# First head of a trunk kernel: pieces in 16 places, a new order of loads, products shared with TensorE, k-steps in two parts

## What is computed

```
a     = silu(c) @ ada_w + ada_b          # shift, scale, gate of each sub-layer
h     = rmsnorm(x, g) * (1 + scale) + shift
q,k,v = split(h @ w_in, 3)               # 8 heads
logit = q @ k.T + rel_table[bucket(j - i)]
```

## Time and profile before

| | us |
|---|---|
| median of 3 runs | 1284.4 (1284.37 to 1286.52) |
| profiled execution, device time | 1283.53 |
| its span in the trace | 1281.7 |
| busy PE | 1234.9 (96%) |
| busy DVE | 695.2 (54%) |
| busy ACT | 562.6 (44%) |
| busy POOL | 528.6 (41%) |

### The profile page before, as it was taken

One profiled execution on the slowest core, in us unless ns is written; L12 is line 12 of the kernel. 1 busy time (PEld: TensorE's weight loads), 2 busy tenths in 40 slices (PEclk: granted clock), 3 DMA queues, 4 the chain that ended last, 5 costly groups with the idle time before them and its releaser, 6 DMA issues.

```text
span 1281.7 us, 16893 instructions
## 1 busy us (share of the span) xinstructions
PE 1234.9 (96%) x5490; PEld 972.4 (76%) x5490; DVE 695.2 (54%) x1175; ACT 562.6 (44%) x899; POOL 528.6 (41%) x265
## 2 busy tenths in 40 slices
PE   4799999989999999999999999999999999999996
PEld 2677777767888888888888777668788888888884
DVE  4756777653676776434444999972533333331002
ACT  4356665663533444342223655663544444442221
POOL 1242333132334444344442677744244444444440
PEclk9799999999999999999999999999999999999999
DMA  9544344422355555234443222202222222232321
GB/s 344 184 145 149 121 140 153 143 99 66 131 196 181 176 183 180 99 109 156 156 166 134 68 66 72 65 27 82 77 89 96 97 90 93 96 109 95 104 87 65
DMA packets 44919, 156.78 MB, mean 122 GB/s; under 512 B 4936, under 2 KB 5192, under 8 KB 44880
## 3 DMA queue, kind: packets, MB, share of 16 engines
q1 hardware_dynamic: 43488, 153.98, 35.4%
q10 hardware_dynamic: 1392, 2.32, 0.6%
HBM read 154.15 MB, written 2.12 MB: 122 GB/s over the span
## 4 chain that ended last, share of the span: by engine, by line
PE 86%; DVE 6%; DMA 3%; issue 2%; ACT 2%; SPq 0%; DVEq 0%; ACTq 0%
PE psum L860 25%; PE psum L862 25%; PE psum L861 25%; PE psum L1126 3%; DMA ada_first<-ada_w 2%; PE psum L895 2%; PE psum L871 1%; DVE pt_lo L1342 1%; DVE psum L1333 1%; PE psum L958 1%; DVE acc L1210 1%; PE psum L907 1%; PE psum L997 0%; PE psum L888 0%; PE psum L985 0%
## 5 line engine op out<-in xcount | busy, mean ns | idle before, releaser
L462 POOL TENSOR_TENSOR w_lo<-w_raw,w_hi 128x1024 fp32r<-128x1024 f32 (+1 forms) x192 | 453.8, 2379 | 707.7 <-ACT w_hi L543 707.7
L860 PE MATMUL psum<-h_hi,w_hi 128*128 128x512 f32 x1152 | 467.1, 405 | 3.8 <-DVE x L1437 2.2
L861 PE MATMUL psum<-h_lo,w_hi 128*128 128x512 f32 x1152 | 449.9, 391 | 0.0
L862 PE MATMUL psum<-h_hi,w_lo 128*128 128x512 f32 x1152 | 449.9, 391 | 0.0
L860 PEld LDWEIGHTS psum<-h_hi,w_hi 128*128 128x128 f32 x1152 | 217.5, 189 | 55.3 <-issue 9.3
L861 PEld LDWEIGHTS psum<-h_lo,w_hi 128*128 128x128 f32 x1152 | 217.3, 189 | 46.9 <-issue 5.3
L862 PEld LDWEIGHTS psum<-h_hi,w_lo 128*128 128x128 f32 x1152 | 216.9, 188 | 46.6
L543 ACT ACTIVATE w_hi<-w_raw 128x1024 fp32r<-128x1024 f32 (+1 forms) x192 | 195.4, 1032 | 73.4 <-DMA w_raw<-w_tiles 73.4
L860 PE MATMUL psum<-a_hi,w_hi 128*128 128x512 f32 x352 | 137.4, 390 | 0.8 <-issue 0.8
L862 PE MATMUL psum<-a_hi,w_lo 128*128 128x512 f32 x352 | 137.0, 389 | 0.0
L861 PE MATMUL psum<-a_lo,w_hi 128*128 128x512 f32 x352 | 137.0, 389 | 0.0
(11 more groups left out here) (184 smaller groups left out, 1361.6 us busy)
## 6 DMA issues: line engine op xcount, KB each, us to landing
w_raw<-w_tiles SPq DMA_DIRECT2D x160, 512.0 KB, 3.3
ada_buf<-ada_w SPq DMA_DIRECT2D x32, 512.0 KB, 3.4
ada_mid<-ada_w SPq DMA_DIRECT2D x32, 512.0 KB, 4.5
w_raw<-w_tiles SPq DMA_DIRECT2D x32, 448.0 KB, 3.1
ada_first<-ada_w SPq DMA_DIRECT2D x16, 512.0 KB, 6.2
ada_late<-ada_w SPq DMA_DIRECT2D x16, 512.0 KB, 4.6
x<-x_in SPq DMA_DIRECT2D x4, 512.0 KB, 10.9
bias<-rel_scratch ACTq DMA_DIRECT2D x1, 2048.0 KB, 8.2
```

Of the source, the lines that this page charges most:

```text
L462: nc.gpsimd.tensor_tensor(w_lo[:, slot, 0:k], w_raw[:, (ph.tile + l) % 2, 0:k], f(w_hi[:, slot, 0:k]), ALU.subtract).then_inc(lo_done, 1)
L860: nc.tensor.matmul(dst, w_hi[:, slot, k], rhs_hi, start=first, stop=False)
L861: nc.tensor.matmul(dst, w_hi[:, slot, k], rhs_lo, start=False, stop=False)
L862: return nc.tensor.matmul(dst, w_lo[:, slot, k], rhs_hi, start=False, stop=last)
```

## The change

It has five parts.
1. The 16 pieces get 16 places (ada_first becomes a list, homes_of_pieces), so no load waits for a buffer. SP issues weight tiles 0 and 1 and x first, then pieces 0 to 7, tables, weight tile 2, pieces 8 to 15, then the bias tiles (moved here from ACT), then tiles 3 to 5.
2. Of chunks 0 and 1, TensorE multiplies k = 1, 3, 5 itself (first_parts, four one-column products for each k, with the piece as weights and a column of cact moving), and DVE the other five. Chunks 2 and 3 stay whole on DVE. DVE now keeps one running sum, in PSUM (FIRST_SUM), and the last addition goes to SBUF. first_product replaces first_ada.
3. DVE adds the squares of x in PSUM, and one 128x512 product sums over partitions instead of eight. ACT splits weight tiles 0 and 1 ahead of the squares, and 1/rms goes to PSUM (OB). The t tiles of the first norm are in PSUM banks 4 and 5.
4. The gain of each half is one instruction (first_gain) instead of two, and first_out takes two chunks in one instruction.
5. Head 0: for k = 0 to 3 all of q, k and v; then the products of chunks 2 and 3, bias tiles 0 and 1; then q and k for k = 4 to 7; then v for k = 4 to 7. DVE does chunks 2 and 3 after the first four norm tiles. All eight bias tiles go through one PSUM bank (FIRST_BIAS), and ACT copies each out (bias_turned) between its other work. The relative bias table's two products follow chunk 1.

```diff
-        first_sums = ((acc[:], v_t[:]), (v_even[:], v_odd[:]))
-        ada_first = at("ada_first", [P, 4, 2, S], F32, qk_base)
+        first_sums = (acc[:], v_t[:], v_even[:], v_odd[:])
...
+        ada_first = [at(f"ada_first{p}", [P, 2, S], F32, o) for p, o in enumerate(homes_of_pieces)]
...
+        PE_PARTS = ((1, 3, 5), (1, 3, 5), (), ())
...
             for t in range(2):
                 load_tile(HEAD, 0, t)
+            for n in range(4):
+                sp.dma_start(x[:, 2 * n:2 * n + 2], x_in[:, 2 * n:2 * n + 2]).then_inc(x_landed[n], 16)
+            for p in range(8):
+                load_first(p)
+            sp.dma_start(tables[:], consts[:, 0:RELS_PAD + 2 * P]).then_inc(consts_in, 16)
+            load_tile(HEAD, 0, 2)
+            for p in range(8, 16):
+                load_first(p)
+            sp.wait_ge(rel_out, 16)
...
+            def first_parts(ch):
+
+                for k in PE_PARTS[ch]:
+                    pe.wait_ge(ada_first_landed[4 * ch + k // 2], 16)
+                    for j in range(4):
+                        nc.tensor.matmul(first_to(ch, j), ada_first[4 * ch + k // 2][:, k % 2, P * j:P * (j + 1)],
+                                         cact[:, k:k + 1], start=(k == PE_PARTS[ch][0]), stop=False)
...
+            first_parts(0)
+            pe.wait_ge(sq_added, DK)
+            nc.tensor.matmul(psum[:, OB], ones[:], rms[:], start=True, stop=True).then_inc(first_sum, 1)
+            first_product(0)
+            first_parts(1)
+            first_product(1)
...
+            def turn_bias(h):
...
+                pe.wait_ge(pt_read, 2 + h)
...
+            for k in range(2, 4):
+                first_qk(k)
+                first_v(k)
+            first_product(2)
+            first_product(3)
+            for h in range(2):
+                turn_bias(h)
+            for k in range(4, DK):
+                first_qk(k)
+                if k < DK - 1:
+                    turn_bias(k - 2)
+            for k in range(4, DK):
+                first_v(k)
+                if k < DK - 1:
+                    turn_bias(k + 1)
...
+            def first_chunk(ch):
...
+                mine = [k for k in range(DK) if k not in PE_PARTS[ch]]
+                for k, after in zip(mine, mine[1:] + [DK]):
...
+                        dve.wait_ge(ada_used, DK * ch + k)
...
+                        V.scalar_tensor_tensor(out=first_sums[ch] if after == DK else psum[:, FIRST_SUM], in0=part,
+                                               scalar=scalar, in1=psum[:, FIRST_SUM], op0=ALU.mult,
+                                               op1=ALU.add).then_inc(ada_used, after - k)
...
+            first_squares()
             dve.wait_ge(act_setup, 1)
             first_chunk(0)
+            first_chunk(1)
             lambda_sums()
...
             norm_tiles(0, 0, DK // 2)
+            dve.wait_ge(h_ready, DK // 2)
+            first_chunk(2)
+            first_chunk(3)
+            first_out(1)
+            first_gain(1)
             norm_tiles(0, DK // 2, DK)
```

More of the change, by code:

```diff
@@ L480, in bias_copy, with mask_add @@
                 nc.gpsimd.tensor_copy(tmps[par][:], tile_of(bias, g)).then_inc(bias_ready, 1)
[L482 to L485, removed]
+            def mask_add(h):
                 pool.wait_ge(pt_read, 3 + h)
@@ L620, in qk_hi_of @@
                 nc.scalar.activation(k_hi[:, par], psum[:, 1], ACT.Copy).then_inc(qk_hi, 1)
+            split_tile(HEAD, 0, 5)
+            bias_turned(4)
             qk_hi_of(0, 0, 0)
-            for h in range(HEADS):
-                act.wait_ge(pt_done, 3 + h)
-                nc.scalar.activation(bias[:, h], psum[:, PT + h % 2], ACT.Copy).then_inc(pt_read, 1)
-                if h == 1:
-                    split_tile(HEAD, 0, 5)
+            for h in range(5, HEADS):
+                bias_turned(h)
             def copy_v(it, c):
@@ L914, in _ @@
-            for ch in range(CH0):
-                first_ada(ch)
+            pe.wait_ge(act_setup, 1)
+            first_parts(0)
[4 more added lines that the diff above has]
+            first_product(1)
+            pe.wait_ge(consts_in, 48)
+            nc.tensor.matmul(psum[0:HEADS, FIRST_BIAS, :], tab[:], onehot[:, 0:S], start=True, stop=True)\
+              .then_inc(pt_done, 1)
@@ new lines, in _, with first_qk @@
+            pe.wait_ge(sc_read, 2)
+            nc.tensor.matmul(psum[0:HEADS, 2, 0:RELS_PAD - S], tab[:], onehot[:, S:RELS_PAD],
+                             start=True, stop=True).then_inc(pt_done, 1)
+            def first_qk(k):
+                pe.wait_ge(h_ready, k + 1)
+                q_last = mm3(psum[:, 0], 0, k, h_hi[:, k], h_lo[:, k], k == 0, k == DK - 1)
+                if k == DK - 1:
+                    q_last.then_inc(q_done, 1)
+                k_last = mm3(psum[:, 1], 1, k, h_hi[:, k], h_lo[:, k], k == 0, k == DK - 1)
+                if k == DK - 1:
+                    k_last.then_inc(k_done, 1)
@@ L936, in head_products @@
                 weights_ready(ph, i2, cc, 3)
[L937 to L938 removed]
+                pe.wait_ge(v_copied, h)
                 for k in range(DK):
@@ L1001, in attention_steps @@
                         10: (lambda: turn_p(3),), 12: (output,), 14: (ada,), 15: (mean_square,)}
-            beside = {DK + k: (lambda h=k: turn_bias(h),) for k in range(DK)}
-            head_products(0, 0, beside)
             with pe.Fori(0, 3) as it:
@@ new lines, in first_out, with two, first_gain @@
+            def first_out(half):
+                def two(t, at_, step):
+                    return t[:, at_:at_ + 2 * step].rearrange("p (a b) -> p a b", a=2)[:, :, 0:4]
+                dve.wait_ge(ada_mm, 2 * (half + 1))
+                V.tensor_tensor(two(mod, DK // 2 * half, DK), first_outs(half),
+                                two(prm, PARAMS["ada_b"] + DK // 2 * half, DK), ALU.add).then_inc(sc_read, 2)
+            def first_gain(half):
+                lo = DK // 2 * half
+                dve.wait_ge(sc_read, 2 * (half + 1))
+                g = PARAMS["norm_g"] + lo
+                V.scalar_tensor_tensor(out=gain[:, 0, lo:lo + 4], in0=mod[:, DK + lo:DK + lo + 4], scalar=1.0,
+                                       in1=prm[:, g:g + 4], op0=ALU.add, op1=ALU.mult).then_inc(dve_step, own.tick())
+                dve.wait_ge(dve_step, own.now())
```

206 lines of the change are left out of this document (109 added, 97 removed).

## The result

The changed kernel is slower than the one before: median 1288.64 us (1286.77 to 1291.27, 10 runs) against 1284.71 us (1282.83 to 1286.58, 10 runs), ratio 1.0031, 95% interval 1.0020 to 1.0042. That is 4.0 us, between 2.6 and 5.4. The forecast was 1283.5 us, with 0.52 on no change and 0.18 on slower. A later comparison of the same two kernels gave 1.0028 (1.0016 to 1.0039).

The account below looks back on a forecast made before the run. PE bounds the kernel, so only an earlier head 1 counts: 71.9 against 72.8, -0.9 us, turns the profiled 1283.53 into 1282.6, and the median 0.9 above it gives 1283.5. The range was 1279.2 to 1287.0.

Parts of the forecast that it names:

- Loads: Start of the kernel: piece 0 lands at 15.9, piece 15 at 37.5, 4 us earlier than before.
- PE before head 0: Chunks 0 and 1 on PE: 32 one-column products at 0.43 plus 1.7, 15.4 us, ending at 31.3.
- first half of the norm: After chunk 1: h complete for k = 0 at 34.3, k = 3 at 38.2; head 0 starts 12.2 us earlier.
- rival 1: Before head 0: PE's clock rises during one-column products, which then cost 0.22; -4.9 us, 1279.5, chance 0.12.
- Chunks 2 and 3: DVE after 38.2: 16 chained instructions 0.78 apart, 12.5 us, ending at 50.7.
- rival 3: Chunks 2 and 3 on DVE: the chain runs at 0.66 an instruction; -2.8 us, 1281.6, chance 0.10.
- The clock in the second half: Second half of head 0: chunk 3's products and first bias tile 1.7 each at low clock, up again at 57.
- Rival 4: Second half of head 0: PE's clock stays low, back later than about 59; +3.1 us, 1287.5, chance 0.18.
- ACT's queue: Before q and k of k = 4: copy 0.60, weight tile 1.04, h_hi 0.76, h_lo 0.81, to 57.4; costs 2 us.
- The rest to head 1: From q and k of k = 4 at 57.4: 14.4 us, and 0.1 for hand-overs, to head 1 at 71.9.
- The mark of before: Head 1's start in the kernel before: 72.8, with three products of v following the last bias product at 71.24.
- rivals 1 to 3: Three faster cases at the start; the second, clock staying high from 45 to 52, gives -2.6 us, 1281.8, chance 0.15.

Follow-up runs that it names:

- experiment 4: Against the changed kernel, ACT splits weight tile 3 before it copies the first bias tile; ratio 1.0032 (1.0018 to 1.0046) to the kernel before.

## Why the prediction was wrong

By its own steps, on the chain's times:

- *Loads, PE before head 0, first half of the norm*: right. 15.9, 31.3 and 34.3 were all met within 0.1, and the end of the first half within 0.3. One-column products kept the low level, and in the run with dense products put ahead PE stayed at 0.50 while it was busy for 17.91 of 18.07 us, so rival 1 is refuted even where its condition was made for it. The Trainium skill ("TensorE: Matmul & The Clock Gate", Part 1) says that the clock rises after a sustained time of activity and that the hardware doesn't count instructions. For one-column products the traces here disagree with that as it stands.
- *Chunks 2 and 3*: this step failed. The trace of before had chained additions only in SBUF, and I took their 0.78 for PSUM, and bounded it by 0.66 and 0.78. They were 0.86 apart, outside my bounds: the row took 14.05 us, not 12.5, and chunk 3 was ready at 51.99, +1.3. That the row is on the path was right, as the interleaved run shows: at the 0.66 of rival 3 it is 3.4 us shorter, and the mark 4.0 earlier.
- *The clock in the second half*: this step failed too. I had it up at 57, and the products of chunk 3 and the first bias tile at 1.7 each. It came at 60.63. The two took 3.86 to the copy (51.99 to 55.85) instead of 3.4 (+0.4), and q and k of k = 4 took 2.48 to the next tile instead of 1.4 (+1.1). I had counted dense time from 52.4 on, but of the 8.59 us at 0.50 PE was idle for 0.9 and held one-column products for 1.9. Rival 4's condition came true ("later than about 59"), and I gave it 0.18. Its price did not: it gave 4.0 for k = 4, k = 6 and their tiles, and the clock cost 1.5 beyond the forecast, because k = 6 and its tile ran at 1.00. That its sum of +3.1 stands near the +2.8 measured at head 1 is luck.
- *ACT's queue*: the copy, weight tile, h_hi and h_lo took 2.96 to q and k of k = 4, not 3.3 (-0.3). But counting this as "costs 2 us" was wrong in another way: taking the weight tile of 1.0 out of it gave back 0.1 at the mark, counted from piece 0.
- *The rest to head 1*: +0.5. The last tiles came 1.81 apart, since all share one bank. The diff shows that, and I had priced the tiles at 0.86 with their products of v beside, not their cycle of product, copy, product.
- *The mark of before*: misread. I let three products of v follow the last bias product; it comes after them, and head 1 starts at 72.10, not 72.8. That is 0.7 us in my favour. My sum should have read 71.9 - 72.1 = -0.2.

Together: -0.2 + 1.3 + 0.4 + 1.1 - 0.3 + 0.5 = +2.8, which is what head 1 shows. DVE's spacing (1.3) and the clock (1.5) weigh about the same, and either alone would have left a loss of about 1 to 1.5 us at head 1. The medians show 0.5 to 0.9 us more than the start does, and the cause of that stays open. The range went wrong for one more reason. Half of it was drawn for cases in which something went better than planned (rivals 1 to 3), and the costs behind DVE's row were each taken at their favourable or middle value, although all of them hang on one event: the later DVE ends, the longer PE idles, and the longer it is slow afterwards.

What the change moved well is there too: head 0 starts 12 us earlier, and the split k-steps save 4.1 against the old order in the profiles. It loses because chunks 2 and 3, which DVE used to add while it waited for pieces, now stand as one chain in front of the second half.

## What to carry to other kernels

Chained accumulation on DVE has a spacing of its own: interleave two sums before you put such a row on the path, here 0.66 instead of 0.86 us an instruction. When work is pulled forward and leaves TensorE idle in front of the next dense stretch, price that stretch at half speed until well into it, and fill the gap up to the last one-column products ahead of it (17 products did in the one profile of it, 8 that ended 0.94 early did not). An instruction taken off the path inside a stretch at the low clock can be worth far less than its length, if the clock's return doesn't move with it (experiment 4). And before two profiles are compared in absolute times, subtract what they already differ by ahead of the edit: 0.86 us here, more than some of the effects looked for.

## What the runs showed of the hardware

- DVE, 128x512 f32, each addition on the result of the last: 0.86 us apart in PSUM, 0.78 in SBUF; on the result of the one before the last, in PSUM, 0.66. The last kind also alternates between two banks; which of the two matters, no run tells.
- A DVE instruction that reads two SBUF operands was held while a POOL instruction that had started before it was under way: 1.91 instead of 0.16 us at 29.42 above, 2.77 instead of 0.75 at 270.98, 2.37 in the kernel before. One that started 0.27 ahead of POOL's was not held (0.75 at 270.54), nor was h_lo at 58.01 in the changed kernel, with one operand in PSUM (0.76, beside a POOL instruction from 57.47 to 59.83).
- One-column products of 128x128 f32 weights took 0.43 us each at granted clock 0.50 and 0.24 at 1.00 (0.95 for four at 45.34), and during 18 us of them the clock didn't rise, even with a dense 128-column product behind every fourth.
- Dense f32 products of 128 columns took 0.24 us each in a row of eight (1.95) and 0.36 in a row of seventeen (6.10), both at granted clock 1.00. Why is open.
- A wait of 2.2 us on TensorE in mid-kernel (294.62 to 296.84) was followed by a stretch at half speed in nine of the ten profiles without products in it, and in none of the four with six. It cost 1.4 us (28.38 against 27.01) to 2.9 us (29.87).
- The moment at which the clock falls and rises differs between executions with the same work: in the changed kernel 50.4 and 60.63 in one profile, 48.2 and 61.85 in another.
